# Up projections that read stored-reversed moving activations backward

## What is computed

```python
h = rms_norm(x, pre_ffn_norm)                # 256 x 2048
# first block: D_FF = 5632
u = causal_dwconv(h @ w_up, conv_w, conv_b)  # w_up 2048 x 11264
gate, up = jnp.split(u, 2, axis=-1)
y = (gelu(gate) * up) @ w_down               # w_down 5632 x 2048
x = x + rms_norm(y, post_ffn_norm)
# second block: D_FF_2 = 8192
u = relu(h2 @ w_up_2)                        # w_up_2 2048 x 8192
y = (u * u) @ w_down_2                       # w_down_2 8192 x 2048
```

## Time and profile before

| | |
|---|---|
| median of 3 runs | 2238.51 us |
| lowest and highest run | 2238.21 and 2238.97 us |
| profiled execution, first to last instruction (span) | 2235.6 us |
| TensorE (matmul) busy | 2215.5 us, 99% |
| VectorE busy | 1416.2 us, 63% |
| ScalarE busy | 1118.0 us, 50% |
| moved from and to HBM | 417.3 MB, 187 GB/s |
| granted TensorE clock, mean | 0.999 |

### The profile page before, as it was taken

How to read it: one execution, slowest core, us unless ns; L and a number is a source line. 1 busy time by engine, 2 the same in 40 slices (tenths; PEclk the granted TensorE clock), 3 DMA queues, 4 the chain that set the end, 5 groups by cost and what they waited for, 6 DMA issues and landing times.

```text
span 2235.6 us, 34152 instructions
## 1 busy us (share of the span) xinstructions
PE 2215.5 (99%) x12721; PEld 1891.4 (85%) x12721; DVE 1416.2 (63%) x1827; ACT 1118.0 (50%) x1567; POOL 65.7 (3%) x95
## 2 busy tenths in 40 slices
PE   8999999999999999999999999999999999999998
PEld 7888888888888888888888888888888888888887
DVE  6466685677776447777566786657666444666545
ACT  5454464555555445555454554545444444444443
POOL 5100000000000000000000000000000000000000
PEclk9999999999999999999999999999999999999999
DMA  9954455566566666666657455566666666666663
GB/s 291 317 180 133 132 167 181 162 190 205 178 201 195 190 194 189 187 188 200 209 147 206 142 162 160 180 195 167 196 191 193 191 196 190 191 192 188 214 192 112
DMA packets 321663, 418.84 MB, mean 187 GB/s; under 512 B 13566, under 2 KB 233048, under 8 KB 320788
## 3 DMA queue, kind: packets, MB, share of 16 engines
q1 hardware_dynamic: 316548, 398.81, 58.3%
q0 software_dynamic: 4720, 16.49, 2.5%
q10 hardware_dynamic: 288, 2.10, 0.3%
HBM read 414.85 MB, written 2.49 MB: 187 GB/s over the span
## 4 chain that ended last, share of the span: by engine, by line
PE 95%; DVE 2%; DMA 1%; issue 1%; ACT 1%; POOL 0%; POOLq 0%; DVEq 0%; SPq 0%; ACTq 0%
PE PS L2024 25%; PE PS L2028 13%; PE PS L1912 10%; PE PS L1911 10%; PE PS L1913 10%; PE PS L2097 5%; PE PS L2368 3%; PE PS L2100 2%; PE PS L2113 2%; PE PS L2115 2%; PE PS L2114 2%; PE PS L2371 2%; PE PS L2381 1%; PE PS L2383 1%; PE PS L2382 1%
## 5 line engine op out<-in xcount | busy, mean ns | idle before, releaser
L2024 PE MATMUL PS<-actu,whi 128*128 128x512 f32 x2432 | 755.6, 392 | 0.0
L2028 PEld LDWEIGHTS PS<-actu,wlo 128*128 128x128 f32 x2432 | 457.1, 188 | 99.9
L1226 DVE TENSOR_TENSOR wlo<-stage,whi 128x1024 fp32r<-128x1024 f32 x296 | 360.4, 1223 | 216.5 <-ACT whi L790 216.2
L1198 DVE TENSOR_TENSOR wlo<-stage,whi 128x1024 fp32r<-128x1024 f32 x245 | 298.9, 1225 | 301.2 <-ACT whi L732 301.2
L2028 PE MATMUL PS<-actu,wlo 128*128 128x256 f32 x2432 | 480.0, 279 | 0.0
L790 ACT ACTIVATE whi<-stage 128x1024 fp32r<-128x1024 f32 x296 | 311.4, 1057 | 304.9 <-PE PS L2028 291.6
L732 ACT ACTIVATE whi<-stage 128x1024 fp32r<-128x1024 f32 x245 | 258.7, 1060 | 344.6 <-PE PS L1913 321.4
L2024 PEld LDWEIGHTS PS<-actu,whi 128*128 128x128 f32 x2432 | 368.4, 188 | 0.6 <-issue 0.4
L1913 PE MATMUL PS<-whi,gT 128*128 128x512 f32 x864 | 336.4, 389 | 0.0
L1912 PE MATMUL PS<-wlo,gT 128*128 128x512 f32 x864 | 336.4, 389 | 0.0
L1911 PE MATMUL PS<-whi,gT 128*128 128x512 f32 x864 | 336.4, 389 | 0.0
(11 more groups left out here) (338 smaller groups left out, 2482.4 us busy)
## 6 DMA issues: line engine op xcount, KB each, us to landing
stage<-in_w_up SPq DMA_DIRECT2D x304, 512.0 KB, 3.9
stage<-in_w_down SPq DMA_DIRECT2D x216, 512.0 KB, 4.2
stage<-in_w_in SPq DMA_DIRECT2D x160, 512.0 KB, 3.8
stage<-in_w_out SPq DMA_DIRECT2D x64, 512.0 KB, 4.2
stage<-in_w_in SPq DMA_DIRECT2D x16, 256.0 KB, 4.0
DQK<-in_cmp_k_w POOLq DMA_DIRECT2D x8, 512.0 KB, 6.6
DQK<-in_cmp_v_w POOLq DMA_DIRECT2D x8, 512.0 KB, 6.3
stage<-in_w_in SPq DMA_DIRECT2D x8, 280.0 KB, 8.3
```

What stands on the lines that cost most here:

```text
L1198: nc.vector.tensor_tensor(wlo[:, s % SPLITS, 0:wd], stage[:, s % STAGES, 0:wd], whi[:, s % SPLITS, 0:wd].bitcast(F32), ALU.subtract).then_ ...
L1226: nc.vector.tensor_tensor(wlo[:, j % SPLITS, :], stage[:, j, :], whi[:, j % SPLITS, :].bitcast(F32), ALU.subtract).then_inc(ev("lo_done"), 1)
L2024: nc.tensor.matmul(o, whi[:, j % SPLITS, at], actu[:, k, :], start=k == 0, stop=False)
L2028: last = nc.tensor.matmul(o[:, S:2 * S], wlo[:, j % SPLITS, at], actu[:, k, 0:S], start=False, stop=k == KC - 1)
```

## The change

The columns of `actu` are stored with the last token first, within the high half and within the low half. `turn_chunks` does it, by an output pattern with step -1 for the turns `n2` and `n4`: the block of token half `t` goes, reversed, to the mirrored place in the bank. The turn `n3` stays as it was. The up projections then read their moving operand from the last column of each half to the first, as a pattern of two runs of 256 columns with step -1 (line 2024) or of one such run (line 2028), and write the bank from its first column to its last as before. What a bank holds at the end is the same as before, and everything behind it is unchanged. No instruction is added or removed, and no semaphore changes.

```diff
@@ turn_chunks @@
-                    last = nc.tensor.transpose(o[:, t * P:(t + 1) * P], x[:, t, at], ident[:, :])
+                    to = o[:, t * P:(t + 1) * P] if turn == "n3" else o[:, S - (t + 1) * P:S - t * P][:, ::-1]
+                    last = nc.tensor.transpose(to, x[:, t, at], ident[:, :])
@@ feat @@
-                                nc.tensor.matmul(o, whi[:, j % SPLITS, at], actu[:, k, :], start=k == 0, stop=False)
+                                both = actu[:, k, :].rearrange("p (a s) -> p a s", a=2)[:, :, ::-1]
+                                nc.tensor.matmul(o.rearrange("p (a s) -> p a s", a=2), whi[:, j % SPLITS, at], both, start=k == 0, stop=False)
@@ feat, second loop @@
-                                last = nc.tensor.matmul(o[:, S:2 * S], wlo[:, j % SPLITS, at], actu[:, k, 0:S],
+                                last = nc.tensor.matmul(o[:, S:2 * S], wlo[:, j % SPLITS, at], actu[:, k, 0:S][:, ::-1],
                                                         start=False, stop=k == KC - 1)
```

## The result

The changed kernel takes 2258.26 us (median; 2257.36 to 2259.14) against 2238.36 us of the kernel before in the same comparison. The ratio is 1.0089, with a 95% interval from 1.0075 to 1.0103: it is slower by about 20 us. The profiled execution of the changed kernel took 2259.14 us, with a span of 2257.3 us. The forecast, no change, was wrong, and so was E, by which the change would not reach the engine; the time lies between the rivals B and C.

The account below looks back on a forecast made before the run. TensorE was taken to bound the kernel. Backward reads, two runs and backward transposes were each put at 0, so 2235.6 us of span plus 2.9 us around it gave 2238.5 us, with a range of 2228 to 2295 us.

Parts of the forecast that it names:

- no change: Whole kernel: the forecast of 2238.5 us, own range 2234 to 2243 us; chance 0.48, with E included.
- E: Up matmul reads: pattern turned round on both sides before issue, reads stay forward, 2238.5 us; chance within the forecast's 0.48.
- Rival B: Up matmuls: the surcharge of 0.015 us per 512 columns doubles, 55 us slower, 2293 us; chance 0.08.
- Rival C: Seams between runs cost up to 12 us, backward-output transposes up to 5.5; 2244 to 2251 us; chance 0.14.
- What bounds the kernel: Whole kernel: TensorE busy 2215.5 of 2235.6 us; a slower up matmul costs its full price; 1216 groups of 0.690 us.
- the moving read with step -1: Up projections, lines 2024 and 2028: reading backward was taken to cost 0, leaving 0.690 us a group.
- 0.015 us surcharge: Up projections' 512-column matmul: 0.230 us against 0.215 for 512 clocks; read as a surcharge of the present forward stream.
- Rival A: Every up matmul: backward stream drops to one column per two clocks, 730 us slower, 2968 us; chance 0.16.
- Rival D: Up matmuls: backward stream smoother, gaining 8 us (2230 us, chance 0.10) or 55 us (2184 us, chance 0.04).

Follow-up runs that it names:

- e1: Kernel before with only the transposes of turns n2 and n4 writing backward, up projections reading forward: 2237.50 us against 2237.17, ratio 0.9999.
- e4: Kernel before with only line 2024's 512-column matmul reading backward, in one run from column 511 to 0: 2258.55 us against 2237.17, ratio 1.0092.
- e7: Kernel before with only `actu` moved by 16 columns (64 bytes), reads forward: 2245.38 us, 696.7 ns per group.
- e15: Kernel before with the weights moved by 16 columns and `actu` by 64, reads forward: 2245.69 us, ratio 1.0036.
- e16: Kernel before with weights, `actu` and all allocated behind moved by 16 columns, reads forward: 2236.92 us, ratio 0.9998.
- e3: Kernel before with only line 2028's 256-column matmul reading backward, in one run: 2248.34 us against 2237.17, ratio 1.0043.
- e2: Kernel before with only line 2024's 512-column matmul reading backward, in two runs: 2250.33 us against 2237.17, ratio 1.0057.
- e9: Kernel before with rows of `actu` 528 columns apart instead of 512, reads forward: 2254.00 us in a single execution, against 2236.45.
- e12: Changed kernel with rows of `actu` 513 columns apart instead of 512, reads backward: 2267.41 us in a single execution; the kernel before took 2236.45.
- e5: Kernel before with only `actu` moved by one column (4 bytes), reads forward: 2265.52 us, 713.4 ns per group.
- e8: Changed kernel with `actu` moved by 16 columns (64 bytes), reads backward: 2263.76 us, 713.3 ns per group in `up1a`.

## Why the prediction was wrong

**What bounds the kernel** was right. TensorE has no slack in these stages, so 16.7 ns per group became 20.3 us without any cover; ScalarE and VectorE only waited longer. The counts, the 1216 groups and the 0.690 us, held.

**The step that failed** is the one on the moving read with step -1, a term put at 0 because "nothing in the rows depends on the direction". It measured 16.7 ns per group, 20.3 us in all, and e1 to e4 place it in the reads of both lines. I had taken a matmul's price as its columns plus a small surcharge that belonged to the stream of moving data. The 0.015 us surcharge of a 512-column matmul isn't a property of that stream. At least in part it is set by where the moving data lie relative to the weights (e7, e15, e16), and the kernel before lies at the best of the uniform places that were measured. As evidence that `actu` streams at an ordinary pace I had the down projections, at 0.227 us for 512 columns; they too read forward, with other tensors on both sides, and could say nothing on what happens when the order of reading changes.

**Rival B** gave a growing surcharge with 55 us; its time was too high by 35 us, and its shape was wrong. It was to grow with the columns in both lines. The changed kernel itself comes near that, with 10.6 and 6.0 ns, but line 2028 alone (e3) cost as much as line 2024 (e2). The mis-sized term is 45 ns per group, measured 16.7. Its direction was right, and so was half of its mechanism: it is a surcharge on the read. **Rival C** fell in both parts: transposes 0 (e1; upper end 5.5 us), and a seam makes a backward read cheaper, not dearer (e2 against e4). The rows that I had read as a seam costing nothing are durations, which overlap like those of the earlier trace rows: 128 of these matmuls start within 1.8 us, 14 ns apart. They gave no price. **Rival A**, the half rate, fell at the first row: 16.7 ns per group, not 600. **Rival D** fell: at no uniform place, and in neither pitch, was backward faster on average than forward; only single chunks of e9 to e12 were.

**The range** (2228 to 2295 us) held the time, but thanks to B and C being counted in it. The chance of 0.48 on no change was too high for a step of which the text itself said that no row was an instance.

**The rule on lines of SBUF** (the Trainium skill, Advanced Engine Details and Errata, Memory Cachelines), by which, as I read it, the direction would make no difference, doesn't agree with 690.0 against 706.7 ns. The rule there on non-contiguous output to PSUM doesn't agree for these transposes: e1 shows no cost for a step of -1. The Trainium skill (SBUF — State Buffer, SBUF: two separate sides) also says that TensorE never waits on anyone; for the other engines the trace of e5 agrees, with 713.0 to 713.5 ns whether they are busy or not. It lists a second, independent read port for the loading of weights. e7, e15 and e16 show that the place of the moving data relative to the weights changes the pace, 690.0 to 696.7 ns, which speaks against two reads that are independent in time.

**What stays open.** That backward reads are dearer because they meet the weight reads at a worse place is a guess: the moving of the weights (e15, e16) was tried with forward reads only. Why the direction costs what it does at a given place is therefore open, and so is why `up2a` in e8 keeps a pace of its own. The opposite case, weights read in the other order with moving data backward, wasn't tried, so whether it is the relative direction of the two reads that counts isn't known. It is also not known which unit of SBUF the period of 64 columns belongs to, and whether the loss by one column (e5) has the same cause.

## What to carry to other kernels

Where TensorE is the bound, the place of a moving operand in SBUF relative to its weights is a parameter of the kernel, worth between 0.2% and 1.2% here (0.2% to 0.4% between places 64 bytes apart), and every edit that moves a tensor or turns the order of a read can change it. Before such an edit is judged, measure it at several places, for example with all places 64 bytes apart within 256 bytes; a difference at one place alone may be that of the place. Here backward was slower at all of these, by 8.9 to 16.7 ns a group. In a kernel in which such a stream has been measured at a good place, leave it alone, and don't price an order of access that no row of the trace shows at nothing.

## What the runs showed of the hardware

- The same four matmuls, forward, at a granted clock of 1.00, take from 690.0 to 713.4 ns by a shift of their moving operand of 0 to 48 columns, with nothing but that place changed. Moving weights and moving operand together restores 690.0.
- Where all chunks lie at one place, most times of a group are on steps: 690.0, 693.3, 696.7, 700.0, 706.7, 713.3 ns are 3.3 ns apart or multiples of it, which is 8 clocks at 2.4 GHz; 702.2 and 715.5 are between them.
- The same instructions at the same places can keep two paces in one execution: 713.3 ns per group in three stages of e8, and 706.7 in the fourth.
- The pace has a period of 64 columns (256 bytes) in the place of the moving operand: in e9 chunks four apart take the same within 0.1 ns, and neighbours from 697.5 to 708.3.
- A transpose with an output of step -1 costs no more than one with step 1: 0.91 us for eight, against 0.94.
- A moving operand in two runs with step -1 is cheaper at this place than the same 512 columns in one run: 700.0 against 706.7 ns per group.
